# Dilated heads: far maxima between the next block's steps, row minima and low parts between the tiles

## What is computed

```python
DIL_CONFIGS = ((128, 1), (512, 4), (2048, 16))      # window, dilation: three groups
# 8 heads per group, head width 64, q and k rotated by rope
s = jnp.where(valid, q . k * D ** -0.5, NEG_INF)     # |offset| <= side, side = 64 in each group
m = jnp.max(s, axis=-1, keepdims=True)
p = jnp.exp(s - m)
o, lse = (p @ v) / den, m + log(den)                 # per group
out = sum_g softmax_g(lse) * o                       # mixture of the three groups
```

## Time and profile before

| what | value |
|---|---|
| median of 3 runs | 3261.86 us (3260.84 to 3262.34) |
| profiled execution | 3261.23 us |
| its span, first to last instruction | 3259.0 us |
| busy: PE, DVE, ACT, POOL | 94%, 39%, 29%, 33% |
| mean granted TensorE clock | 0.958 |

### The profile page before, as it was taken

The page is one execution under the profiler, slowest core; times in us unless marked ns, Lnnn a source line. Parts: engine busy times, 40 slices in busy tenths (PEclk is TensorE's granted clock), DMA queues, the critical chain, the costliest instruction groups (busy, mean ns, idle before and its releaser), DMA issues.

```text
span 3259.0 us, 39528 instructions
## 1 busy us (share of the span) xinstructions
PE 3047.7 (94%) x14770; PEld 2469.9 (76%) x14770; DVE 1279.6 (39%) x1618; ACT 951.7 (29%) x1527; POOL 1079.4 (33%) x857
## 2 busy tenths in 40 slices
PE   7989998999989999999996799999999999989998
PEld 6777776888868888878876466699787777768886
DVE  2673665211230000013354688710656666640122
ACT  3223555201220000011132456611444444420011
POOL 2432110444424444444432100055333232334443
PEclk8999999999989999999998799999999999989999
DMA  3111000211321111121121000033222222231122
GB/s 123 38 61 36 23 24 21 92 48 45 107 84 45 48 46 47 48 94 48 48 77 51 13 14 13 10 121 115 67 74 71 76 59 79 58 136 48 45 103 84
DMA packets 101806, 199.17 MB, mean 61 GB/s; under 512 B 14272, under 2 KB 31424, under 8 KB 101184
## 3 DMA queue, kind: packets, MB, share of 16 engines
q1 hardware_dynamic: 62496, 115.90, 12.0%
q10 hardware_dynamic: 39200, 81.72, 7.5%
HBM read 153.53 MB, written 31.46 MB: 57 GB/s over the span
## 4 chain that ended last, share of the span: by engine, by line
PE 79%; DVE 13%; ACT 4%; issue 2%; DMA 1%; POOL 1%; ACTq 0%; DVEq 0%; POOLq 0%; SPq 0%; PEldq 0%
PE ps L289 31%; PE ps L271 14%; PE ps L305 12%; PE ps L1595 7%; PE ps L931 3%; PE ps L962 1%; DVE mla_nm L904 1%; DVE mla_ptl L895 1%; ACT ps L871 1%; PE ps L947 1%; DVE norm_xn L426 1%; PE ps L949 1%; PE ps L948 1%; PE ps L1918 1%; PE ps L1253 1%
## 5 line engine op out<-in xcount | busy, mean ns | idle before, releaser
L2609 POOL TENSOR_TENSOR wh<-raw,zeros 128x512 fp32r<-128x512 f32 x426 | 462.7, 1086 | 2122.6 <-PE ps L289 713.0
L2611 POOL TENSOR_TENSOR wl<-raw,wh 128x512 fp32r<-128x512 f32 x426 | 616.4, 1447 | 33.4
L289 PE MATMUL ps<-hth,wh 128*128 128x512 f32 x1216 | 483.3, 397 | 11.1 <-ACTq L177 11.1
L289 PE MATMUL ps<-hth,wl 128*128 128x512 f32 x1216 | 482.4, 397 | 0.0
L289 PE MATMUL ps<-htl,wh 128*128 128x512 f32 x1216 | 482.2, 397 | 0.0
L271 PE MATMUL ps<-wh,hth 128*128 128x512 f32 (+3 forms) x768 | 283.6, 369 | 6.7 <-ACTq L247 4.1
L305 PE MATMUL ps<-hth,wh 128*128 128x512 f32 x704 | 287.8, 409 | 2.1 <-DVE fox_vl L1144 2.1
L271 PE MATMUL ps<-wl,hth 128*128 128x512 f32 (+3 forms) x768 | 282.2, 367 | 0.0
L305 PE MATMUL ps<-hth,wl 128*128 128x512 f32 x704 | 282.1, 401 | 0.0
L271 PE MATMUL ps<-wh,htl 128*128 128x512 f32 (+3 forms) x768 | 282.1, 367 | 0.0
L305 PE MATMUL ps<-htl,wh 128*128 128x512 f32 x704 | 281.3, 400 | 0.0
(11 more groups left out here) (393 smaller groups left out, 5437.7 us busy)
## 6 DMA issues: line engine op xcount, KB each, us to landing
raw<-in_stream_dram SPq DMA_DIRECT2D x426, 256.0 KB, 2.6
dil_stg<-dil_stg ACTq DMA_DIRECT2D x96, 128.0 KB, 2.4
vd_dram<-dil_stg ACTq DMA_DIRECT2D x8, 768.0 KB, 4.4
dil_sz<-vd_dram ACTq DMA_DIRECT2D x12, 512.0 KB, 4.4
norm_x<-in_x_dram ACTq DMA_DIRECT2D x8, 512.0 KB, 9.9
heads_raw<-heads_dram ACTq DMA_DIRECT2D x8, 512.0 KB, 7.6
norm_x<-in_x_dram ACTq DMA_DIRECT2D x1, 4096.0 KB, 16.0
x_dram<-norm_x ACTq DMA_DIRECT2D x8, 512.0 KB, 2.6
```

Source lines behind the costliest of these rows:

```text
L289: ins = nc.tensor.matmul(ps[:, bank + half, :], w[:, j % 2, c:c + P], a[:, k, HALF * half:HALF * half + HALF], start=first and q == 0, sto ...
L2609: nc.gpsimd.tensor_tensor(wh[:, s, :], raw[:, s, :], zeros[:].to_broadcast([P, HALF]), ALU.add).then_inc(w_hi, 1)
L2611: nc.gpsimd.tensor_tensor(wl[:, s, :], raw[:, s, :], wh[:, s, :], ALU.subtract).then_inc(w_split, 1)
```

## The change

1. **Far maxima.** `maxima(s)` no longer stands by itself ahead of `block(s+1, 0)`. Its parts come between that block's steps: pairs 0 and 1 after step 1, pair 2 after step 2, pair 3 after step 3, the rows after step 4. Steps 5 to 7 follow, then the scores. The block waits for the last near maximum in place of the last far one. For head 7, which has no next block, the parts run one after the other as before.
2. **Minima.** Only `r` stays ahead of the tiles. `r.1` comes after `lo` of tile 1, `r.2` after `lo` of tile 2. `scores(s, 4)` now waits for `r.2`.
3. **Low part of group 2's keys.** `kl.2` comes after `lo` of tile 3; `scores(s, 8)` waits for it, and `scores(s, 0)` no longer does.
4. **Last third of the values** (even heads): ACT's `vh.2` comes after `p` of tile 5, DVE's `vl.2` after `lo` of tile 6; TensorE waits for it ahead of tile 8.
5. **The cosine product** `t1` of the next head comes after `lo` of tile 7.

```diff
 # lists of steps
-    split(s, 2, first + rest), f"sz{s}", f"row{s}", f"table{s}", thirds(s, 2, "vh"))
+    split(s, 2, first + rest), f"sz{s}", f"row{s}", f"table{s}")
-    [f"mx{s}.{m}" for m in maxima[4:]], f"ql{s}.2", f"kl{s}.2", f"r{s}", f"r{s}.1", f"r{s}.2", thirds(s, 2, "vl"))
+    [f"mx{s}.{m}" for m in maxima[4:]], f"ql{s}.2", f"r{s}")
+def between(s, n):
+    return flat({1: [f"r{s}.1"], 2: [f"r{s}.2"], 3: [f"kl{s}.2"], 6: thirds(s, 2, "vl"), 7: [f"t1{s + 1}.0"] if s < 7 else []}.get(n, []))
...
 # ACT
-    v_load(s, 2)
-    v_high(s, 2)
+    v_load(s, 2)
...
     a.did(nc.scalar.activation(at, at, ACT.Exp), f"p{s}.{n}")
+    if n == 5:
+        v_high(s, 2)
...
 # DVE
-    low(s, 2)
+    low_queries(s, 2)
     a.wait(dve, f"row{s}")
     v.did(tt(places(self.E[96:97, 0, :]), places(row0), row12, ALU.min), f"r{s}")
-    for g in (1, 2):
-        v.did(tt(self.E[96:97, g, :]..., places(row0), row12, ALU.min), f"r{s}.{g}")
-    v_low(s, 2)
...
 for s in range(self.HEADS):
-    if s < 7:
-        first(s + 1, 0)
     for n in range(self.SLOTS):
         ...                                    # lo{s}.{n}
+        if n in (1, 2):
+            row_by_class(s, n)                 # r{s}.{n}
+        if n == 3:
+            low_keys(s, 2)
+        elif n == 6:
+            v_low(s, 2)
+        elif n == 7 and s < 7:
+            first(s + 1, 0)
...
 # TensorE
     elif g == 0:
-        v.wait(pe, f"mx{s - 1}.b3")
+        v.wait(pe, f"mx{s - 1}.n3")
...
-def maxima(s):
-    a.wait(pe, f"c{s}.2")
-    if s:
-        v.wait(pe, f"on{s - 1}")
-    for j in range(4):
+def maxima(s, k):
+    if k == 1:
+        a.wait(pe, f"c{s}.2")
+        if s:
+            v.wait(pe, f"on{s - 1}")
+    for j in {1: (0, 1), 2: (2,), 3: (3,)}.get(k, ()):
         if j >= 2:
             v.wait(pe, f"mx{s}.b{j - 2}")
         ...
+    if k != 4:
+        return
     v.wait(pe, f"mx{s}.b3")
...
     if n == 0:
         v.wait(pe, f"r{s}")
-        v.wait(pe, f"kl{s}.2")
+        v.wait(pe, f"kl{s}.1")
     if g and n == self.last[g - 1] + 1:
-        v.wait(pe, f"r{s}.{g}")
+        v.wait(pe, f"r{s}.2" if g == 1 else f"kl{s}.2")
...
-maxima(0)
 for s in range(self.HEADS):
     if s < 7:
-        block(s + 1, 0)
+        block(s + 1, 0, lambda k, s=s: maxima(s, k))
+    else:
+        for k in range(1, 5):
+            maxima(s, k)
     scores(s, 0)
     scores(s, 1)
     if s % 2 == 0:
-        v.wait(pe, f"vl{s // 2}.2")
+        v.wait(pe, f"vl{s // 2}.1")
     for n in range(self.SLOTS):
+        if n == 8 and s % 2 == 0:
+            v.wait(pe, f"vl{s // 2}.2")
         ...
     if s < 7:
         ...
         gate(s + 1)
-        maxima(s + 1)
```

More of the change, by code:

```diff
@@ L2048, in __init__ @@
                     [f"zv{j}.{t}" for j in range(1, 4) for t in range(NT)], "x0.0", prep_a(0),
-                    *[flat([f"x{s + 1}.0"] if s < 7 else [], *[[f"hi{s}.{n}", f"p{s}.{n}"] for n in N], f"ev{s}",
+                    *[flat([f"x{s + 1}.0"] if s < 7 else [], *[[f"hi{s}.{n}", f"p{s}.{n}"] + (thirds(s, 2, "vh") if n == 5 else []) for n in N], f"ev{s}",
                            prep_a(s + 1) if s < 7 else []) for s in H]))
@@ L2052, in __init__ @@
                     "t10.0", prep_v(0),
-                    *[flat([f"t1{s + 1}.0"] if s < 7 else [], [f"lo{s}.{n}" for n in N], f"cmb{s}",
+                    *[flat(*[flat(f"lo{s}.{n}", between(s, n)) for n in N], f"cmb{s}",
                            prep_v(s + 1) if s < 7 else ["rc7", "on7"]) for s in H]))
@@ L2320, in low, with low_queries @@
                 def low(s, g):
+                    low_queries(s, g)
+                    low_keys(s, g)
+                def low_queries(s, g):
                     a.wait(dve, f"qh{s}.{g}")
@@ L2324, in low, with low_keys @@
                     v.did(tt(self.G[64:128, g, :], R[0:64, :], self.G[0:64, g, :], ALU.subtract), f"ql{s}.{g}")
+                def low_keys(s, g):
+                    R = self.rotated(s, g)
                     a.wait(dve, f"kh{s}.{g}")
@@ L2367, in prepare, with row_by_class @@
                         v.did(nc.vector.tensor_reduce(self.nm[:, 2 * j:2 * j + 2], ps[:, bank:bank + 2, 0:384], AX, ALU.max, negate=True), f"mx{s}.b{j}")
-                    low(s, 2)
+                    low_queries(s, 2)
                     a.wait(dve, f"row{s}")
-                    places = lambda T: T.rearrange("a (v b m) -> a v b m", b=2, m=4)
-                    row0, row12 = ps[0:1, 6:8, :].rearrange("p a b -> p (a b)"), self.XS[0:1, :].rearrange("a (b m v) -> a v b m", b=2, m=4)
                     v.did(tt(places(self.E[96:97, 0, :]), places(row0), row12, ALU.min), f"r{s}")
-                    for g in (1, 2):
-                        v.did(tt(self.E[96:97, g, :].rearrange("a (m b v) -> a v b m", b=2, m=4), places(row0), row12, ALU.min), f"r{s}.{g}")
-                    v_low(s, 2)
+                places = lambda T: T.rearrange("a (v b m) -> a v b m", b=2, m=4)
+                row0, row12 = ps[0:1, 6:8, :].rearrange("p a b -> p (a b)"), self.XS[0:1, :].rearrange("a (b m v) -> a v b m", b=2, m=4)
+                def row_by_class(s, g):
+                    v.did(tt(self.E[96:97, g, :].rearrange("a (m b v) -> a v b m", b=2, m=4), places(row0), row12, ALU.min), f"r{s}.{g}")
                 first(0, 0)
```

## The result

| | before | changed |
|---|---|---|
| median of 20 runs each | 3259.47 us | 3264.34 us |
| ratio, 95% interval | | 1.0017 (1.0010 to 1.0024) |
| span of the profiled execution | 3259.0 us | 3263.2 us |
| mean granted TensorE clock | 0.958 | 0.961 |

The changed kernel is slower by 0.10% to 0.24%, 4.9 us or 0.15% between the medians. That is a small loss, clear of zero, of the size that the prediction counted as no change. The forecast was 3264 us, with a sum of plus 2.0 us on the kernel before's own profiled time.

The account below looks back on a forecast made before the run. TensorE, 94% busy, was taken as the bound, losing time to idle and low clock at the far maxima. 3261.2 - 47.6 + 40.1 + 2.5 + 7.0 = 3263.2 us, plus 0.6 for the median: 3264 us, range 3247 to 3282.

Parts of the forecast that it names:

- Gain of part 1: Gate's last matmul to next projection's copy: 15.7 us per head without idle, seven heads 157.7 to 110.1 us, gaining 47.6 us.
- near +4.6: Far maxima in head 2: first maximum done about 4.6 us after the gate's end, before step 2 ends at +5.7.
- the weights: nothing: GpSimd's work on the weights for the block's steps: no cost expected, as GpSimd is 33% busy.
- The tight place: Far maxima between block steps: last maximum done at +9.6 us, step 4 ends at +9.8, 0.2 us of cover.
- The cover of `r`: Behind the rows: 4.2 us of block hide the row copy and `r`, 3.1 us, with 1.1 us to spare.
- Loss of part 2: Tile loop: tiles end late behind `r.2`, even heads 5.6 us, odd heads 5.9 us, 40.1 us in all.
- 7.0 of clock: Tile loop: TensorE's clock falls near 2488 after idle, costing 1.0 us per head (bounds nothing to 2.7), 7.0 us in all.
- Head 7: 2.5 us: Last head, without swap: two minima between its `lo` steps make it about 2.3 us late, 2.5 with the clock.
- The low clock through the tiles: Rival, tile loop: clock stays low, each head loses 3.4 us in place of 1.0, total 3281 us; chance 0.20.
- The tiles did not catch up: Rival, tile loop: tiles catch up, 2.5 us per head come back, total 3246 us; chance 0.12.
- the price of the cosine product: Rival, moved minima: each costs 1.23 us like the cosine product, not 1.95, total 3254 us; chance 0.05.
- rival 4: Far maxima still wait between the steps: 3 us per head of the gain go, total 3285 us; chance 0.08.

Follow-up runs that it names:

- the swap moved: Changed kernel with ACT's swap of the next head ahead of tile 6's exponential in place of tile 3's: 3258.01 us, 0.9996 of the kernel before.
- the filler: Changed kernel plus unread matmuls, 14 ahead of the wait for tile 4's scores, 8 ahead of `second` of tile 3: 3263.12 us, 1.0015 of the kernel before.
- both: Changed kernel with swap ahead of tile 6 and only the 14 unread matmuls ahead of the wait for tile 4's scores: 3248.49 us, 0.9972 of the kernel before.
- the run with the minima ahead: Changed kernel with `r.1` and `r.2` back ahead of the tiles, directly behind `r`: 3217.17 us, 0.9875 of the kernel before.
- the run with one more: Changed kernel with `r.1` done twice, between the low parts of tiles 1 and 2: 3278.66 us, 1.0063 of the kernel before.

## Why the prediction held, point by point

- **The sum.** Plus 2.0 us were forecast, and 4.9 measured between the medians (4.2 between the spans). The time itself, 3264 against 3264.34 us, is closer than that by luck: the forecast stood on a median of 3 runs, 3261.86 us, and the 20 runs have 3259.47. The two large terms came out 1.4 us smaller (the gain) and 0.3 us larger (the loss) than worked out.
- **What bounds the kernel.** TensorE's idle and low clock in the far maxima: shown, by the stretch that shrank from 22.5 to 15.9 us on average (157.7 and 111.5 us over seven).
- **Gain of part 1: 47.6 us; measured 46.2.** Odd heads took 15.43 us against my 15.7, even ones 16.31: the wait before pair 2, 0.61 us of idle in the view and 0.9 us of the path. (Seven times 15.7 is 109.9 us, not 110.1; the 0.2 us change nothing.) There the first maximum was done 6.4 us behind the gate's end, not "near +4.6", because two low parts ahead of it had become longer. In the kernel before they took 1.22 and 1.23 us at this place (L2326 and L2331, from 2458.71 and 2459.96). DVE's and GpSimd's timelines of the changed kernel, head 2:

```profile
2456.66 1.95 DVE L2338 TENSOR_TENSOR dil_f<-dil_stg,dil_f 64x1024 fp32r<-64x1024 f32 x1
2458.64 2.21 DVE L2343 TENSOR_TENSOR dil_vl<-dil_sz,dil_vh 128x1024 fp32r<-128x1024 f32 x1
2460.77 1.81 DVE L2379 TENSOR_REDUCE dil_nm<-ps 128x2 fp32r<-128x768 f32 x2
...
2455.88 1.65 POOL L2635 TENSOR_TENSOR wh<-raw,zeros 128x512 fp32r<-128x512 f32 x1 [3.66 <-PE ps L305]
2457.61 2.16 POOL L2637 TENSOR_TENSOR wl<-raw,wh 128x512 fp32r<-128x512 f32 x1
```

  GpSimd splits the weights as the block's steps begin. Before, they began behind the far maxima, and it split at 2468.42; now it splits beside these low parts. So "the weights: nothing" was the step that failed here, for 1.7 us of DVE and 0.9 us of the path in each even head. The tight place I had named, the last maximum against step 4, held. The cover of `r` held as well: it ended 1.2 us ahead of the copy.
- **Loss of part 2 in the loop: 40.1 us and 7.0 of clock, 47.1; measured 47.4.** In head 2 the exponential of tile 3 came 6.0 us later relative to the copy (10.84 against 4.82), where 5.9 were worked out, and the odd heads lost more than the even ones, by 0.6 us in head 1 against the even heads of equal low clock, where I had 0.3. Heads with 3.4 us of low clock lost 5.9 and 6.5 us, 0.3 and 0.6 above my figures for the high clock; heads 3, 4 and 5 lost 0.7, 2.5 and 0.9 us on top. So the clock's share was 4.1 us, inside my bounds of 0 to 2.7 us per head, and the share at the high clock 43.3. I had 7.0 and 40.1: that their sum was met to 0.3 us is luck, two errors of 3 us that cancel.
- **The reason for it was only half right.** The prediction says that the queue behind `swap` is the point and that the clock's cost "just fills the gap up to tile 3: nothing". Both sentences describe the changed kernel well. But they make one of two nearly equal waits the cause: the runs with the swap moved, with the filler and with both show that queue and clock are worth 5.4 and 3.0 us alone and 15.9 together. The other 31.5 us of the 47.4 need neither: 24.1 us of them lie ahead of tile 3's `second`, in TensorE's own wait for `r.2`, which the prediction names only beside the queue, and 7.4 us behind it. The root of all of it is the end of `r.2`, as the run with the minima ahead and the run with one more show from both sides.
- **Head 7: 2.5 us; measured 2.6.** The agreement says little: with the swap moved, an edit that doesn't touch head 7, the same stretch took 20.6 us in place of 19.1.
- **Rivals.** The low clock through the tiles came in one head of seven (head 4: 10.2 us low, 24.64 us). The tiles did not catch up. The minima took 1.87 to 1.97 us in their new place, so the price of the cosine product, 1.23 us, and with it the 1.22 us that the Trainium skill (VectorE: DVE Perf Modes, section "The TRN2 errata") gives for such an operation, does not hold for them; no run here tells whether the one partition, the permuted order or the operand in PSUM is the reason. The far maxima waited 4.8 us in all in place of 20.4: rival 4 came for 0.9 us of the path per even head, against its 3.

Not tried: the wait of `swap` for `r.2` with the minima reading another buffer than `XS`, which would take the queue's wait away at its root.

## What to carry to other kernels

A wait is worth what the other waits beside it leave: before a cause is named for a stall, count every way from the late step to the work that is late, and take away one, the other and both. Small work on one engine is not free filling: with two minima of 1.9 us between tiles of 1.4 us each, the loops of seven heads were 47 us longer, because a queue, a product and a clock hung on the second; with the same two minima ahead of the tiles and all else equal they were 6 us longer. And when a change has a gaining and a losing part, run the parts alone: here the better kernel was the change without one of its five edits.

## What I had not expected of the hardware

DVE beside GpSimd: the changed kernel's stage has 60 low parts with both inputs in SBUF, of the keys (L2338), of the queries (L2333) and of the values (L2343). The 32 with no GpSimd operation beside them took 1.20 to 1.23 us, and so did one with 0.07 us of it. Of the keys' and values', the 12 that ran beside one for more than 1 us took 1.95 to 2.21 us. The queries' were hit less: 7 with 0.75 us of GpSimd beside them took 1.22 us, one with 1.16 us took 1.24 and 7 with 1.38 us took 1.45. GpSimd was longer too: its 128x512 addition took 1.65 us in head 2 and 1.04 us at its place in the kernel before, and its subtraction (L2637) 2.16 us beside a low part of the queries and 1.28 to 1.31 us alone or beside a DVE operation that reads PSUM. The Trainium skill (GPSIMD Engine Reference, Specifications) says that the two share their way into SBUF and contend when a VectorE instruction has two SBUF inputs. By that rule, a low part, whose inputs both lie in SBUF, and GpSimd's work hold each other up, and the trace agrees; which of the two pays, and how much, differs from case to case, and nothing here shows why. No run moved GpSimd's work alone, so this is read from these cases and not tried. The minima's 1.87 us has another cause: they took it with GpSimd idle.

In these loops the clock's low stretches came in lengths of 3.4, 6.8 and 10.2 us, and behind the same idle of 3.5 us heads 0 to 2 and 6 took no longer than with the clock kept high (22.1 and 22.75 us against the filler run's 22.3 and 22.9), while head 4 took 2.5 us more than head 2, in one and the same run. The Trainium skill (TensorE: Matmul & The Clock Gate, Part 1) says that the moment of a clock change shifts from run to run with where the matmuls fall against the monitor's free-running rhythm. By that rule, equal heads may differ, and the trace agrees: 22.1 and 24.6 us. Filling the idle with matmuls that nobody reads made the seven loops alike to within 0.1 us among the even and among the odd heads.
